# A delta rule's triangular inverse in three steps of factor four, and expert slots counted inside the first gate product

## The reference, cut to what matters

```
A   = tril(K K^T * decay, -1) * beta
sol = solve(I + A, [v * beta, k * beta * exp(G)])
o   = q_dec @ state + (tril(q k^T) * decay) @ (u - w @ state)
state = state * g_last + k_tail^T @ (u - w @ state)
```

## Time and profile before

| what | value |
|---|---|
| runs of the kernel before | 2433.41 us median of 3 (2429.43 to 2441.47) |
| the profiled execution's own time | 2439.54 us |
| its span in the profile | 2437.7 us |
| PE busy in the span | 2210.5 us (91%) |
| DVE busy | 1255.5 us (52%) |
| ACT busy | 475.6 us (20%) |
| POOL busy | 119.6 us (5%) |

### The profile page before, as it was taken

The page is one execution under the profiler, slowest core; times in us unless marked ns, Lnnn a source line. Parts: engine busy times, 40 slices in busy tenths (PEclk is TensorE's granted clock), DMA queues, the critical chain, the costliest instruction groups (busy, mean ns, idle before and its releaser), DMA issues.

```text
span 2437.7 us, 24059 instructions
## 1 busy us (share of the span) xinstructions
PE 2210.5 (91%) x9014; PEld 1351.1 (55%) x9014; DVE 1255.5 (52%) x2135; ACT 475.6 (20%) x874; POOL 119.6 (5%) x111
## 2 busy tenths in 40 slices
PE   6998788999999899988999899999998699999783
PEld 3444344888888644434444478788875333333231
DVE  4674564566575531885757757776535421212113
ACT  1125441111000101134333334341001000000002
POOL 0000000000000000000000022220000000001000
PEclk8999888999999999899999999999998799999996
DMA  7136501422222222110122000022243699999994
GB/s 262 35 116 213 207 1 42 105 100 73 69 95 78 93 96 70 42 69 1 69 69 70 0 1 1 1 95 79 101 187 115 263 415 426 426 426 426 426 425 193
DMA packets 97290, 364.67 MB, mean 150 GB/s; under 512 B 10396, under 2 KB 19281, under 8 KB 84625
## 3 DMA queue, kind: packets, MB, share of 16 engines
q1 hardware_dynamic: 86337, 340.62, 36.3%
q0 software_dynamic: 8720, 20.89, 2.3%
q10 hardware_dynamic: 2112, 1.57, 0.2%
HBM read 357.00 MB, written 17.57 MB: 154 GB/s over the span
## 4 chain that ended last, share of the span: by engine, by line
PE 71%; DVE 14%; DMA 7%; ACT 4%; issue 3%; POOL 0%; SPq 0%; DVEq 0%; ACTq 0%; POOLq 0%
PE bank L670 50%; PE bank L1373 8%; PE bank L1144 5%; PE bank L734 3%; DVE mem L2010 2%; DMA mem<-in_w_gate 2%; PE bank L904 2%; DMA mem<-in_w_down 2%; DMA mem<-in_w_up 2%; ACT mem L2326 1%; PE bank L779 1%; DVE mem L1951 1%; DVE mem L1950 1%; ACT L2490 1%; PE bank L1353 1%
## 5 line engine op out<-in xcount | busy, mean ns | idle before, releaser
L670 PE MATMUL bank<-mem 128*128 128x256 f32 (+6 forms) x4976 | 1536.0, 471 | 47.7 <-ACT mem L2326 10.9
L670 PEld LDWEIGHTS bank<-mem 128*128 128x128 f32 (+2 forms) x4976 | 934.8, 195 | 594.1 <-issue 449.0
L1373 PE MATMUL bank<-mem 128*64 128x512 f32 x1248 | 283.8, 610 | 33.0 <-DMA mem<-in_w_gate 11.5
L2326 ACT ACTIVATE mem<-bank 128x512 f32<-128x512 f32 (+5 forms) x294 | 163.1, 555 | 430.0 <-PE bank L734 185.2
L1373 PEld LDWEIGHTS bank<-mem 128*64 128x64 f32 x1248 | 94.4, 140 | 212.7 <-issue 199.4
L734 PE MATMUL bank<-mem 128*128 128x128 f32 (+1 forms) x820 | 138.6, 302 | 70.7 <-DVE mem L1609 24.2
L734 PEld LDWEIGHTS bank<-mem 128*128 128x128 f32 (+1 forms) x820 | 102.9, 152 | 123.6 <-DVE mem L1609 37.2
L1144 PE MATMUL bank<-mem 128*128 128x128 f32 x1280 | 157.5, 276 | 3.9 <-ACT mem L2326 3.3
L1144 PEld LDWEIGHTS bank<-mem 128*128 128x128 f32 x1280 | 149.8, 192 | 9.3 <-ACT mem L2326 4.9
L2262 DVE TENSOR_TENSOR mem<-mem,bank 128x512 f32<-128x512 f32 x19 | 13.1, 690 | 272.5 <-PE bank L1373 203.6
L2439 ACT ACTIVATE mem<-bank 128x512 f32<-128x512 f32 (+1 forms) x50 | 29.1, 581 | 381.8 <-PE bank L670 380.1
(11 more groups left out here) (320 smaller groups left out, 1518.7 us busy)
## 6 DMA issues: line engine op xcount, KB each, us to landing
mem<-in_w_gate SPq DMA_DIRECT2D x37, 2048.0 KB, 25.4
mem<-in_w_up SPq DMA_DIRECT2D x37, 2048.0 KB, 24.5
mem<-in_w_down SPq DMA_DIRECT2D x36, 2048.0 KB, 25.8
mem<-in_w_in SPq DMA_DIRECT2D x18, 2048.0 KB, 7.8
mem<-in_w_ada SPq DMA_DIRECT2D x12, 2048.0 KB, 7.9
mem<-in_w_out SPq DMA_DIRECT2D x4, 2048.0 KB, 12.8
mem<-in_w_ple_gate SPq DMA_DIRECT2D x2, 2048.0 KB, 7.9
mem<-in_w_br_att SPq DMA_DIRECT2D x2, 2048.0 KB, 7.8
```

The source lines that it names most:

```text
L670: last = pe.matmul(o, l, r, start=(i == 0), stop=(i == len(pairs) - 1))
L1373: last_ = pe.matmul(o[here, :], lhs[:, k, here], w[:, k, cols], start=(k == 0), stop=(k == kk - 1))
L2326: C(act.activation(dst, src, ACT.Copy), act_free)
```

## The change

A level now joins two of the old levels: three levels of factor four instead of six of factor two. With X the inverse of the diagonal blocks and L the masked part of A, M = X L has M^4 = 0, and the new inverse is X - M(X - M(X - M X)). A level takes five steps: turn X (ACT copies XT); quad L^T XT, which is M^T (ACT copies it); and three quads with M^T as the stationary side, each followed by a DVE subtraction from X (W in the code is `u`; the last of the three at the last level has the sides exchanged and gives XT). On DVE, `decays_differ` and `decays_bound` stay at step 9 and `decays_end` moves from step 13 to 15. `halfway` in the expert's product is `all_slots`. A is not turned any more: POOL masks A itself, and XT of the first level comes from PE and ACT instead of DVE. There are 19 steps. Beside it, `z_rows(2)` moves ahead of step 1 of group 1, `all_slots` moves into the middle of block 0's gate product, and the first block's slots are made ahead of the order of experts. The sizes of the constants stay as they are.

```
@@ PE
-    elif step == 1:
-        to_wait(a_ready[g])
-        turn("act", [B["A"][:, h, :] for h in range(HG)])
...
+    lv, phase = divmod(step - 1, 5)
...
+    elif step < 16 and phase == 0:
+        if lv == 0:
+            to_wait(x0_ready[g])
+        else:
+            pe.wait_ge(dve_free, updated[g])
+        turn("act", [X(h) for h in range(HG)])
+        if lv == 1:
+            four("dve", q_, k_)
+    elif step < 16 and phase == 1:
+        to_wait(level_ready[g])
+        pe.wait_ge(act_free, turned_at[g])
+        four("act", lambda h: B[f"L{lv % 2}"][:, h, :], XT)
+        if lv == 0:
+            turn("dve", [k_(h) for h in range(HG)])
+        if lv == 1:
+            turn("act", [B["qk"][:, h, :] for h in range(HG)])
+    elif step < 16 and phase == 2:
+        pe.wait_ge(act_free, turned_at[g])
+        four("dve", M_T, X)
+    elif step < 16 and phase == 3:
+        pe.wait_ge(dve_free, updated[g])
+        four("dve", M_T, W)
+        if lv == 0:
+            turn("dve", [v_(h) for h in range(HG)])
+        if lv == 1 and ch < NT - 1:
+            gains_along_rows(g)
+    elif step < 16:
+        pe.wait_ge(dve_free, updated[g])
+        if lv < 2:
+            four("dve", M_T, W)
+        else:
+            four("dve", W, M_T)
...
     for g, ch, step in DELTA_ORDER:
         delta_step(g, ch, step)
+        if (g, step) == (1, 0) and ch == 0:
+            z_rows(2)
         if (g, step) == (1, 1) and ch == 0:
-            z_rows(2)
             z_rows(3)
@@ PE, block 0 of the experts
+    for k in range(kk):
+        if halfway is not None and k == kk // 2:
+            halfway()
+        last_ = pe.matmul(o, lhs[:, k, :], ws[0][:, k, cols], start=(k == 0), stop=(k == kk - 1))
@@ DVE
     elif step == 1:
         V(tt(B["X"], B["A"], over(const("level0"), HG), ALU.mult))
-        V(tt(B["X"], over(ident, HG), B["X"], ALU.subtract))
-        dve.wait_ge(act_free, mark["AT", g, ch])
-        V(tt(B["XT"], B["AT"], over(const("level0_t"), HG), ALU.mult))
-        V(tt(B["XT"], over(ident, HG), B["XT"], ALU.subtract), x0_ready[g])
+        V(tt(B["X"], over(ident, HG), B["X"], ALU.subtract), x0_ready[g])
...
+    elif step < 16 and (step - 1) % 5 > 1:
+        V(tt(B["X" if phase == 4 else "u"], B["X"], full_bank(), ALU.subtract), dve_free)
+        if step == 4:
+            V(tt(B["v_b"], full_bank(), inner(beta[:, ch, gh], P), ALU.mult), dve_free)
...
+        if ch and step in (3, 5, 8, 10, 13, 15):
+            result_norm(g, ch - 1, (3, 5, 8, 10, 13, 15).index(step))
...
+    slots_from(take()[:, 0:1], 0, 1, dve_free)
     my_place = const("token")[:, 0:1]
     V(ts(at_place, place_of, my_place, None, ALU.is_equal))
...
     V(dve.tensor_copy(order_i[:, 0:1], order_f[:, 0:1]), experts_known)
...
-    slots_from(take()[:, 0:1], 0, 1, dve_free)
@@ POOL
-    if ch < NT and step % 2 == 0 and 2 <= step < 14:
+    if ch < NT and step in (1, 6, 11):
+        lv = step // 5
         if lv == 0:
-            pool.wait_ge(act_free, mark["AT", g, ch])
-        if lv >= 1:
-            pool.wait_ge(act_full, mark["T", g, ch, max(lv - 2, 0)])
-        mask = const("levels_t", 6)...
-        pool.tensor_tensor(delta[g][f"L{lv % 2}"], delta[g]["AT"], mask, ALU.mult)
+            pool.wait_ge(a_ready[g], ch + 1)
+        if lv == 2:
+            pool.wait_ge(act_full, mark["T", g, ch, 0])
+        mask = const("levels", 3)...
+        pool.tensor_tensor(delta[g][f"L{lv % 2}"], delta[g]["A"], mask, ALU.mult)
```

More of the change, by code:

```diff
@@ L59 @@
 HG = 4
-STEPS = 17
+STEPS = 19
 BIG = -3e38
@@ L98 @@
     ("cos", NT * 16), ("sin", NT * 16), ("chunk_mask", 512), ("causal_mask", 512),
-    ("level0", 128), ("level0_t", 128), ("levels_t", 6 * 128)])
+    ("level0", 128), ("levels", 3 * 128), ("spare_rows", 4 * 128)])
 COLS, N_COLS = layout([
@@ L144, in shape_constants @@
     put("level0", level(0))
-    put("level0_t", level(0).T)
-    put("levels_t", np.concatenate([level(n).T for n in range(1, 7)], axis=1))
+    put("levels", np.concatenate([level(n) | level(n + 1) for n in (1, 3, 5)], axis=1))
     rel = np.arange(640) - 511
@@ L1189, in delta_step @@
                     return
+                X, XT, M_T, W = (lambda h, n=n: B[n][:, h, :] for n in ("X", "XT", "AT", "u"))
+                lv, phase = divmod(step - 1, 5)
                 if step == 0:
                     four("dve", k_, k_)
-                elif step == 1:
-                    to_wait(a_ready[g])
-                    turn("act", [B["A"][:, h, :] for h in range(HG)])
-                    mark["AT", g, ch] = done["act"]
-                elif step < 14 and step % 2 == 0:
-                    lv = step // 2 - 1
+                elif step < 16 and phase == 0:
                     if lv == 0:
                         to_wait(x0_ready[g])
+                    else:
+                        pe.wait_ge(dve_free, updated[g])
+                    turn("act", [X(h) for h in range(HG)])
+                    turned_at[g] = done["act"]
+                    if lv == 1:
+                        four("dve", q_, k_)
+                        mark["qk", g, ch] = done["dve"]
+                elif step < 16 and phase == 1:
                     to_wait(level_ready[g])
[L1201 to L1204, removed]
+                    pe.wait_ge(act_free, turned_at[g])
+                    four("act", lambda h: B[f"L{lv % 2}"][:, h, :], XT)
                     turned_at[g] = done["act"]
@@ L1209, in delta_step @@
                     if lv == 1:
[L1210 to L1214, removed]
                         pe.wait_ge(dve_free, mark["qk", g, ch])
@@ L1236, in delta_step @@
                     mark["wT", g, ch] = done["act"]
-                elif step == 15:
+                elif step == 17:
                     pe.wait_ge(act_free, mark["wT", g, ch])
@@ L1380, in expert_block @@
                 every = slice(0, EFF)
[L1381 to L1384, removed]
+                expert_product(banks[2][:, :], xgT[:, n % 2, :, :], weights_here(n, "gate", wide_at), every, KD,
+                               all_slots if n == 0 else None).then_inc(gate_full, 1)
                 expert_product(banks[3][:, :], xgT[:, n % 2, :, :], weights_here(n, "up", wide_at), every, KD)\
@@ L2520, in delta_step @@
                         result_root(g)
[L2521 to L2525, removed]
-                    four_out(B["u"])
-                    if step == 8:
-                        four_out(B["qkT"])
+                elif step < 16 and step % 5 == 1:
+                    four_out(B["XT"])
                     if step == 6 and ch:
                         result_root(g)
-                elif step == 11 and ch < NT - 1:
+                elif step < 16 and step % 5 == 2:
+                    four_out(B["AT"])
+                    if step == 7:
+                        four_out(B["qkT"])
+                elif step == 10 and ch < NT - 1:
                     decays(g, ch + 1)
-                elif step == 14:
+                elif step == 16:
                     if ch:
@@ L2543, in _ @@
                 delta_step(g, ch, step)
+                if (g, step) == (1, 0) and ch == 0:
+                    z_out(1, 2)
                 if (g, step) == (1, 1) and ch == 0:
-                    z_out(1, 2)
                     z_out(1, 3)
```

48 lines of the change are left out of this document (19 added, 29 removed).

## The result

| what | before | after |
|---|---|---|
| median of ten runs each | 2436.14 us | 2448.31 us |
| lowest and highest | 2429.43 to 2441.47 | 2443.40 to 2451.45 |
| ratio, 95% interval | 1 | 1.0052 [1.0040, 1.0063] |
| the profiled execution's own time | 2439.54 us | 2444.65 us |
| its span | 2437.7 us | 2442.8 us |

PE, ACT and POOL are busy for less time than before. So nothing was added to the engine that looked like the bound: PE is idle 240.8 us of its span for 227.2 before.

What follows compares the result with a forecast made beforehand. Bounds: in the experts' stage the weight stream's start, in the delta stage the walk of PE, DVE, ACT and POOL over the steps. Terms summed to +11.2 us on 2439.54, or 2450.7; stated as median 2445, range 2426 to 2456.

Steps and rivals of the forecast that it cites:

- case (e): Whole kernel: the author's own forecast, 2440 to 2450 us; chance 0.42.
- Part 3, the turn of a chunk: Turn between chunks: gate tile 6.1 us later (T: end of A of group 0); with clock, +23.5 us over three.
- The clock: Gate tiles after the three turns of chunks: half clock, 2.3 us each, less the 1.7 already paid.
- Part 2, the middles: Step 2 to next step 0: saved turns return as waits; -3.3, -0.3, -0.3, +0.3 us in chunks 0 to 3.
- Part 4, z_rows(2): Start of chunk 0: the moved z product fills PE's 3.67 us wait; -1.3 us at half clock.
- Part 5, the slots: Experts' block 0: slots made sooner, gather 1 lands 3.8 us earlier and the clock holds; -7.4 us.
- (b): Turn of a chunk: masks and first inverse do not meet and the clock holds; -11, 2423 us; chance 0.15.
- (a): Turn of a chunk: masks and first inverse collide, but the clock holds; +4, 2437 us; chance 0.17.
- (c): Experts' stage: gather 1 gains nothing; +18.6, 2452 us; chance 0.13.
- (d): Delta stage: longer waits, blocked operations at full length (+3) or slower middles (+8); about 2450 us; chance 0.13.

Runs made afterwards that it cites:

- experiment 1: The kernel before with both edits of the slots alone, delta rule as before: 2428.61 us, ratio 0.9973.
- e4: The changed kernel with gate tile and both z products of chunk 0 ahead of step 1 of group 0: 2418.43 us, ratio 0.9933.
- e8: The kernel before with gate tile and z products ahead of step 1 of both groups: 2447.00 us, ratio 1.0046.
- experiment 2: The changed kernel with the slots as in the kernel before: 2450.64 us, ratio 1.0069.
- Experiment 4: The changed kernel with POOL's first masks behind the first inverse of both groups: 2431.55 us, ratio 0.9993.
- Experiments 6 to 10: Changed kernel: tile early 0.9933, masks late too 0.9928, DVE side work moved too 0.9880; kernel before: tile early 1.0046, side work moved 0.9985.
- e7: The changed kernel with PE kept busy by unread products in its waits for X in chunks 1 to 3: 2444.46 us, ratio 1.0045.

## Why the prediction was right, point by point

The forecast was 2445 us, +11.2 on the profiled execution, "same" 0.47 and "slower" 0.45. It came out at 2448.31, with a ratio right at the bound of 0.5%: case (e), at its slow edge. The +12.2 between the medians is close to +11.2, but in part by luck: the terms of the walk came out at +14.9 (delta stage +21.1 for 18.6, slots -6.2 for -7.4), and untouched code gave some of it back.

- **Part 3, the turn of a chunk**, carried the sum and held. I walked X of group 0 to T+4.3 and X of group 1 to T+7.6; the rows give 1519.26 and 1522.61, T+4.3 and T+7.6. The stretch between the middles grew by 6.6, 6.7 and 6.6 us where I had 6.1; the rest is the turn of X of group 1 at half clock (1.12 for 0.66). The alternation of DVE and POOL came as taken. The Trainium skill ("SBUF — State Buffer", "SBUF: two separate sides") has the loser fully blocked for the whole instruction, which with 1.27 and 0.69 us gives an estimate of 1.96 for a blocked operation. The eight L2047 took 1.64 on average, and in the alternation DVE operations started 1.68 us apart (1517.62, 1519.30). So the trace bears out the exclusion, and not its full length, as the earlier trace rows had said.
- **The clock** was put at 2.3 us a tile less 1.7, that is +5.2. The chain shows the three tiles 3.6 us longer (9.03, 7.90, 9.03 for 6.88, 6.88, 8.58), and the turn at half clock adds about 0.46 us three times: 5.0 in all. The fall came after all three waits; one tile of the three recovered sooner. So part 3's 23.5 was met (19.9 and 3.6), with the turn's share of the clock in the other term.
- **Part 2, the middles.** Chunk 3 has +0.6 for +0.3, chunks 1 and 2 have +0.3 each for -0.3. The mis-sized term is chunk 0: -3.3 in the walk, -1.5 measured. There PE's busy time fell by 1.77 us (40.95 to 39.18) where six turns at 0.44 had been counted as 2.64, and PE is idle 2.59 us, where the walk left it about 1.6. All four middles together are 0.3 us shorter for the 3.6 of the walk.
- **Part 4, z_rows(2)**: -2.2 for -1.3, since the second z product took 7.84 us in the chain and not the 9.1 of half clock.
- **Part 5, the slots.** Gather 1 was issued 3.0 us sooner behind the reduction, not 3.8, because the first half of the gate product took 6.77 us for my 5.9. The wait fell to 2.23 us (1.7 predicted), and the clock held in the profiled execution. Gather 1 itself took 11.27 us for the 10.75 that I had kept. That gives -6.2 for -7.4; experiment 1 has -6.6 by its ratio, for the whole kernel.
- **What no step of mine had.** Between the last gate tile and the slots the code is untouched, yet the stretch took 270.7 us before and 265.5 after. Over all kernels it is 268.7 to 271.3 us with the old delta part and 265.5 to 268.1 with the new. In it PE's first products after a wait for weights took 7.17 us after where they had taken 8.86, and a turn 1.09 where it had taken 1.97: the clock that follows a wait, again. It is not tied to the delta part alone: e4, with the new one, has 8.86 us, and e8, with the old one, 7.17. Why it falls less often there I did not test, and it stays open. The shorter stretch goes with 21.1 us in the delta stage being only 17 in experiment 2's ratio.
- **The rivals.** (b) fell with the trace: masks and first inverse meet every time. Experiment 4 makes its first half true, and there the clock fell all the same (tiles of 7.85, 8.94 and 7.79 us): 0.9993, not the 0.996 (2423 us) that (b) gives with the clock held. (a) fell with the clock, (c) with the gather. (d) was there in small: the middles came out 3.3 us longer than walked in all, where (d) had up to 8.

The prediction's weak point was not a number. It took the turns saved as worth nothing because "they come back as waits", and left it at that. Experiments 6 to 10 show that the waits belonged to the places of two things that the change left where they were, the gate tile and the side work, and that 1.7% lay between the change as made and the change with both moved and the masks late.

## What to carry to other kernels

When a change shifts a dependency from one operand to the next (here from A to X made of A), the independent work that used to hide the old wait stands in the wrong place: move it ahead of the new wait first, and judge the change after that. A form with fewer levels, each a longer chain of product and subtraction, saved its time here only when nothing else stood in the queue between them, so look for the idle stretches of the engine that subtracts and put the side work there. And an engine that is idle over 90% of the time (POOL) should not start as early as it can while an operation with both operands in SBUF is on the critical path of DVE.

## What the runs showed of the hardware

- A DVE operation of 128x512 float32 with both operands in SBUF, 0.69 us alone, took 1.64 us beside POOL's masks and ended 0.55 us after the mask; issued with a mask half done it took 1.13. The masks, 1.27 us alone, took 5.13 for three. With one operand in a PSUM bank both kept their time (0.69 and 1.27 us).
- The clock after a wait is not a function of the wait's length alone. In block 0, after 2.23 us it held (down product 7.13 us), after 2.21 and 2.48 us it fell (9.35 and 9.26 us). Behind the last gate tile, PE's first products after a wait of 1.87 us took 8.86 us in the kernel before and 7.17 in e7. At the turn of a chunk it had fallen after 4.38 us (turn at 1.11 us for 0.66). Forecasts that hang on it need both values in the range.
- Products put into a wait, whose results nobody used, held the clock: all gate tiles at 6.88 us. The ratio gives the whole kernel 2 us for it, the trace 6 in the delta stage.
